# First block's heads: two latent tiles normalized ahead, the last tile's split and stores on two engines each, and attention that waits for its operands head by head

## The reference

```python
proj = jnp.einsum('bsd,dc->bsc', h, w_in[l])
cq, ckv, kr = proj[..., :o1], proj[..., o1:o2], proj[..., o2:o3]      # 384, 256, 32 columns
dq, dk, dv = proj[..., o3:o4], proj[..., o4:o5], proj[..., o5:]       # 8 heads of 64 each
q  = einsum('bsr,rc->bsc', rms_norm(cq, g_q[l]), w_uq[l])             # 8 heads of 96
kv = einsum('bsr,rc->bsc', rms_norm(ckv, g_kv[l]), w_ukv[l])          # 8 heads of 64 + 64
# rotations of the last 32 columns of q, of kr, and of the first 16 of each head of dq and dk
out_a = mla_attention(q, k, v)
out_b = dilated_attention(partial_rope(dq), partial_rope(dk), dv)
```

## Time and profile before

| | |
|---|---|
| time, median of 3 runs | 4233.45 us (4229.98 to 4238.81) |
| profiled execution's own time | 4241.43 us |
| its span, first to last instruction | 4239.6 us |
| busy PE, DVE, ACT, POOL | 3618.3, 2504.6, 2043.9, 782.3 us |
| mean granted clock of TensorE | 0.926 of full |
| `stage_heads1`, first load to the next stage's first | 324.55 to 477.02 us |
| first attention's loads to its first matmul | 477.02 to 490.96 us |
| first matmul of the second block's first attention | 2289.95 us |

### The profile page before, as it was taken

How to read it: one execution, slowest core, us unless ns; L and a number is a source line. 1 busy time by engine, 2 the same in 40 slices (tenths; PEclk the granted TensorE clock), 3 DMA queues, 4 the chain that set the end, 5 groups by cost and what they waited for, 6 DMA issues and landing times. The chain is left out here.

```text
span 4239.6 us, 68993 instructions
## 1 busy us (share of the span) xinstructions
PE 3618.3 (85%) x24823; PEld 2980.6 (70%) x24823; DVE 2504.6 (59%) x4458; ACT 2043.9 (48%) x3629; POOL 782.3 (18%) x464
## 2 busy tenths in 40 slices
PE   3996699988659999759997899965979997899759
PEld 3993488776548888648886677854768786788647
DVE  1204366433577888557653777755647745877655
ACT  1315455751047777552223666654442225666542
POOL 0212200020026665413340000002013430000020
PEclk7998799999679999879998999997989998999989
DMA  7126643412869999643234434341233326244413
GB/s 278 58 72 225 195 119 68 87 42 74 342 255 388 396 396 396 228 162 102 88 103 115 137 78 88 65 98 54 79 131 113 109 85 190 56 92 92 85 56 96
DMA packets 425466, 624.68 MB, mean 147 GB/s; under 512 B 118693, under 2 KB 281157, under 8 KB 424101
## 3 DMA queue, kind: packets, MB, share of 16 engines
q1 hardware_dynamic: 413216, 576.55, 43.8%
q0 software_dynamic: 8096, 30.02, 2.4%
q10 hardware_dynamic: 3812, 13.69, 1.0%
HBM read 486.20 MB, written 133.97 MB: 146 GB/s over the span
## 5 line engine op out<-in xcount | busy, mean ns | idle before, releaser
L1230 ACT ACTIVATE aa_prob<-aa_ps,aa_nm 128x256 f32<-128x256 f32 (+2 forms) x680 | 473.5, 696 | 287.0 <-DVEq L1181 248.9
L1101 PE MATMUL aa_ps<-aa_op 128*128 128x512 f32 (+2 forms) x1408 | 376.0, 380 | 177.9 <-DVEq L1189 130.4
L1180 DVE TENSOR_REDUCE aa_nm<-aa_ps 128x1 f32<-128x1280 f32 (+1 forms) x252 | 345.9, 1373 | 227.4 <-PE aa_ps L1101 214.6
L1101 PEld LDWEIGHTS aa_ps<-aa_op 128*128 128x128 f32 x1408 | 235.8, 193 | 298.7 <-issue 158.6
L1989 PE MATMUL pr_ps<-pr_wH,hT_part 128*128 128x512 f32 (+1 forms) x1120 | 429.5, 383 | 0.0
L1721 ACT ACTIVATE ex_high<-ex_ring 128x2048 fp32r<-128x2048 f32 x192 | 368.7, 1920 | 98.3 <-PE ex_pg L1697 43.2
L1767 DVE TENSOR_TENSOR ex_ring_part<-ex_ring,ex_high 128x2048 fp32r<-128x2048 f32 x144 | 377.1, 2619 | 52.4 <-ACTq L1722 40.6
L1131 PE MATMUL aa_po<-aa_pT,aa_op 128*64 128x128 f32 x5552 | 388.7, 282 | 0.0
L1989 PE MATMUL pr_ps<-pr_wH,x_sb_part 128*128 128x512 f32 x896 | 361.1, 403 | 24.4 <-DVEq L2065 20.5
L1112 PE MATMUL aa_ps<-ident,aa_prob 128*128 128x128 f32 x2776 | 376.4, 279 | 6.1 <-ACTq L1234 5.9
L1989 PE MATMUL pr_ps<-pr_ws_part,x_sb_part 128*128 128x512 f32 x896 | 354.0, 395 | 0.0
(11 more groups left out here) (298 smaller groups left out, 6984.9 us busy)
## 6 DMA issues: line engine op xcount, KB each, us to landing
ex_ring<-in_w_gate SPq DMA_DIRECT2D x64, 1024.0 KB, 9.9
ex_ring<-in_w_up SPq DMA_DIRECT2D x64, 1024.0 KB, 8.3
ex_ring<-in_w_down SPq DMA_DIRECT2D x64, 1024.0 KB, 8.0
aa_op<-z_d SPq DMA_DIRECT2D x120, 320.0 KB, 9.5
z_d<-pr_zT SPq DMA_DIRECT2D x120, 256.0 KB, 2.8
pr_ws<-in_w_in SPq DMA_DIRECT2D x14, 2048.0 KB, 8.7
mod_w<-in_w_ada SPq DMA_DIRECT2D x10, 2048.0 KB, 13.4
rt_mw<-in_w_ada SPq DMA_DIRECT2D x8, 2048.0 KB, 16.5
```

What stands on the lines that cost most here:

```text
L1101: mm = tensor.matmul(ps[:, base[h] + at:base[h] + at + m], q.bitcast(F32R), kk.bitcast(F32R), start=i == 0, stop=i == len(ab) - 1)
L1180: vector.tensor_reduce(most, scores[:, 0:g_.count[t]], AX.X, ALU.max, negate=True)
L1230: scalar.activation(prob[:, base[h] + c0:base[h] + c1], ps[:, base[h] + c0:base[h] + c1], ACT.Exp, bias=nm[:, h % 4:h % 4 + 1], scale=-1.0 ...
```

## The change

In `stage_heads1` the scaled latents get a second buffer, and tile t + 2 is normalized in pass t: ACT's `latents(t + 2)` stands behind `turned_latents(t + 1)` and ahead of `finished(t - 1)`, DVE's behind `heads(t)`. `load(1)` moves ahead of the gains and weights. For the last tile DVE makes the LOW parts of groups 1 and 3, and ACT issues the stores of groups 2 and 3. In `stage_attention` each head of a unit has a semaphore of its own.

```diff
-            c_n, c_T = sb("cn", [P, Q_RANK + KV_RANK]), sb("cT", [P, CR, P])
+            c_n, c_T = sb("cn", [P, 2, Q_RANK + KV_RANK]), sb("cT", [P, CR, P])
...
                     if t == 0:
                         load(0)
+                        load(1)
...
-                        load(1)
                     if t + 2 < ST:
...
-                            sp.wait_ge(low, (t - 1) * 4 + m + 1)
+                            if t < ST:
+                                sp.wait_ge(low, (t - 1) * 4 + m + 1)
+                            elif m < 2:
+                                sp.wait_ge(low if m == 0 else low_last, (ST - 1) * 4 + 1 if m == 0 else 1)
+                            else:
+                                continue
...
-                    if t:
-                        dve.wait_ge(cT_ps, t)
+                    if t >= 2:
+                        dve.wait_ge(cT_ps, t - 1)
...
                 latents(0)
                 dilated(0)
+                latents(1)
                 for t in range(ST):
-                    if t + 1 < ST:
-                        latents(t + 1)
                     heads(t)
+                    if t + 2 < ST:
+                        latents(t + 2)
                     if t + 1 < ST:
                         dilated(t + 1)
+
+                for m in (1, 3):
+                    dve.wait_ge(high, (ST - 1) * 4 + m + 1)
+                    o = outT[m][:, (ST - 1) % 2]
+                    vector.tensor_tensor(o[:, LOW].bitcast(F32R), o[:, LOW], o[:, HIGH], ALU.subtract)
+                    dve.drain().then_inc(low_last, 1)
...
                 latents(0)
+                latents(1)
                 act.wait_ge(gains, 32)
                 turned_latents(0)
                 for t in range(ST):
-                    if t + 1 < ST:
-                        latents(t + 1)
                     key_value(t)
                     if t + 1 < ST:
                         turned_latents(t + 1)
+                    if t + 2 < ST:
+                        latents(t + 2)
                     if t:
                         finished(t - 1)
                 finished(ST - 1)
+                tok = slice((ST - 1) * P, ST * P)
+                for m, dst in ((2, q_dil), (3, k_dil)):
+                    act.wait_ge(low if m == 2 else low_last, (ST - 1) * 4 + 2 if m == 2 else 2)
+                    for x in (HIGH, LOW):
+                        act.dma_start(dst[x].rearrange("(c p) s -> p c s", p=P)[:, :, tok], outT[m][:, (ST - 1) % 2, x])\
+                            .then_inc(t_st[(ST - 1) % 2], 16)
...
-                    for m in range(4):
+                    for m in range(4) if t < ST - 1 else (0, 2):
...
-        loaded = [sum(16 * g_.n_loads for g_, _ in units[u % 2:u + 1:2]) for u in range(len(units))]
+        loaded = [sum(8 * g_.n_loads for g_, _ in units[u % 2:u + 1:2]) for u in range(len(units))]
...
-                    if t == 0 and j == 0:
-                        pe.wait_ge(ld[u % 2], loaded[u])
+                    if t == 0:
+                        pe.wait_ge(ld[u % 2][j], loaded[u])
```

More of the change, by code:

```diff
@@ L651, in stage_heads1 @@
             sem(n + s) for s in ("_sq", "_cn", "_cps", "_csb", "_kvup", "_qup", "_qout", "_qk", "_dil", "_tr"))
-        ev, cp, high, low = (sem(n + s) for s in ("_ev", "_cp", "_high", "_low"))
+        ev, cp, high, low, low_last = (sem(n + s) for s in ("_ev", "_cp", "_high", "_low", "_lowlast"))
         v_st, t_st = ([sem(f"{n}_{s}{j}") for j in range(2)] for s in ("vst", "tst"))
@@ L724, in latents @@
                     rstd(dve, var, root, ss[:, :], rt[:, :], r[:, :], tm[:, :], t + 1)
-                    if t:
-                        dve.wait_ge(cT_ps, t)
-                    vector.tensor_scalar(c_n[:, 0:Q_RANK], x[:, 0:Q_RANK], r[:, 0:1], None, ALU.mult)
-                    vector.tensor_scalar(c_n[:, Q_RANK:], x[:, Q_RANK:Q_RANK + KV_RANK], r[:, 1:2], None, ALU.mult)
+                    if t >= 2:
+                        dve.wait_ge(cT_ps, t - 1)
+                    vector.tensor_scalar(c_n[:, t % 2, 0:Q_RANK], x[:, 0:Q_RANK], r[:, 0:1], None, ALU.mult)
+                    vector.tensor_scalar(c_n[:, t % 2, Q_RANK:], x[:, Q_RANK:Q_RANK + KV_RANK], r[:, 1:2], None, ALU.mult)
                     dve.drain().then_inc(cn, 1)
@@ L840, in latents @@
                     for c in range(CR):
-                        mm = tensor.transpose(cps[:, c, :], c_n[:, c * P:(c + 1) * P], ident[:, :])
+                        mm = tensor.transpose(cps[:, c, :], c_n[:, t % 2, c * P:(c + 1) * P], ident[:, :])
                     mm.then_inc(cT_ps, 1)
@@ L980, in tiles_at @@
             return [m for m in range(M) if 2 * m + lag[2 * m] + behind == s]
-        ld, lv = ([sem(f"{name}_{s}{b}") for b in range(2)] for s in ("ld", "lv"))
+        lv = [sem(f"{name}_lv{b}") for b in range(2)]
+        ld = [[sem(f"{name}_ld{b}{j}") for j in range(2)] for b in range(2)]
         ex0, tr0 = sem(f"{name}_ex0"), sem(f"{name}_tr0")
@@ L1026, in operands @@
                         for x in (HIGH, LOW):
-                            yield qT(g_, b, x, j, slice(0, g_.dq)), q_[x][:, j, :]
-                            yield kT(g_, b, x, j, slice(0, g_.dq)), k_[x][j]
+                            yield j, qT(g_, b, x, j, slice(0, g_.dq)), q_[x][:, j, :]
+                            yield j, kT(g_, b, x, j, slice(0, g_.dq)), k_[x][j]
                         continue
@@ L1032, in operands @@
                         rows = slice(m * g_.dq, (m + 1) * g_.dq)
-                        yield qT(g_, b, 0, j, rows), q_[qx][:, j, :]
-                        yield kT(g_, b, 0, j, rows), k_[kx][j]
+                        yield j, qT(g_, b, 0, j, rows), q_[qx][:, j, :]
+                        yield j, kT(g_, b, 0, j, rows), k_[kx][j]
                         if g_.dq == 64:
-                            yield kL(g_, b, j, rows), k_[LOW][j]
+                            yield j, kL(g_, b, j, rows), k_[LOW][j]
             def value_operands(u):
@@ L1055, in loads @@
                 def loads(u):
-                    for dst, src in itertools.islice(operands(u), 0, None, 1 if u else 2):
-                        sp.dma_start(dst, src).then_inc(ld[u % 2], 16)
+                    for j, dst, src in itertools.islice(operands(u), 0, None, 1 if u else 2):
+                        sp.dma_start(dst, src).then_inc(ld[u % 2][j], 16)
                     for dst, src in value_operands(u):
@@ L1234, in exponentials @@
                         act.drain().then_inc((ex0, ex)[x], 1)
-                for dst, src in itertools.islice(operands(0), 1, None, 2):
-                    act.dma_start(dst, src).then_inc(ld[0], 16)
+                for j, dst, src in itertools.islice(operands(0), 1, None, 2):
+                    act.dma_start(dst, src).then_inc(ld[0][j], 16)
                 for s in slots:
```

## The result

The changed kernel takes 4264.64 us (median of 5 runs, 4258.12 to 4270.21), the kernel before 4234.98 us (5 runs, 4229.98 to 4239.14). The ratio is 1.0064, with a 95% interval of 1.0052 to 1.0075: 27 us slower, 22 to 32 (the two medians are 29.7 us apart). The profiled execution took 4260.41 us.

A forecast was written before the change was run, and what follows sets the result against it. Before, ACT's list plus its wait for transposes bounds a pass; changed, a load-store loop does. 36.3 + 6.2 - 2.1 - 0.9 + 0 - 7.8 = +31.7 on 4233.45 gives 4265 us; 8-in-10 range 4250 to 4277.

The forecast's parts named there:

- The closed loop: Stage's tile passes: squares wait for a load behind stores that wait for ACT; four passes of 24.4 us, +36.3 us.
- The choice of 5.20: In the loop: ACT's copies of `finished` taken as 5.20 us, not 4.13, because PE would have stood before them.
- The margin before: Stage's passes before the change: the tile load was hidden with some 2 us to spare.
- The start: Stage's start: weights land later behind `load(1)`, root waits for DVE's heads, copies slower as PE cools; +6.2 us.
- The last two passes: Tiles 5 and 6, with no latents ahead: passes of 14.0 and 11.4 us, -2.1 and -0.9 us.
- The tail: Last tile's split and stores: the DMA queue is already full, so 0 us.
- Head by head: Attention: head 0 starts earlier but only one block of scores is won at each of three waits; -7.8 us.
- The rival on the other side: Loop: pipelining works if the load lands under 9 us after the HIGH copies; -15 to -20 us, 4215; chance 3%.
- Half hidden: Loop: shorter wait through faster issues from a rested queue; passes 18 to 20 us, 4238 to 4248; chance 9%.
- The dearer loop: Loop: PE's products at half clock add 1 to 3 us a pass; 4270 to 4280; chance 12%.

The follow-up runs named there:

- e3_tail_only: The kernel before with only the last tile's LOW-part subtractions and stores split over two engines each: 4237.85 us, ratio 1.0000.
- e4_loop_only: The kernel before with only the latents two tiles ahead and tile 1's load ahead of the weights: 4275.21 us, ratio 1.0089.
- e9_five_buffers: The changed kernel with five tile buffers, loads ahead of stores, squares before turned latents, DVE's latents before heads, start order mostly restored: 4217.64 us, ratio 0.9949 to kernel before.
- e5_behind: The changed kernel with ACT's squares and root of tile t + 2 behind the copies of tile t - 1: 4226.74 us, ratio 0.9980 to the kernel before.

## Why the prediction was right, step by step

- **The closed loop** was the step that carried it: 24.4 us a pass in four passes, +36.3. Measured 24.35, +36.1. Taken apart: issue of the load 10.60 for 10.61, from there to the squares 6.61 for 6.6, squares and root 1.83 for 1.91, copies 5.31 for 5.20. (The four terms of the forecast add up to 24.32, which it rounds up to 24.4.) The choice of 5.20 held: of the two lengths in rows 3, 4.13 came at a granted clock of 1.00 and 5.20 at 0.50, and in the slow pass it was 0.54. The wait itself was put too short, 8.2 to 8.7 us against a stated 4 to 8, because ACT was ready for the squares 8.5 to 9.0 us after the HIGH copies, the early end of what was allowed; in a pass that the load sets, this costs nothing. The margin before was smaller than the forecast's 2 us: the load of tile 5, issued at 389.81, took 6.7 us and was wanted at 397.39, 0.9 us later. That it is this loop, and not DVE's heads or the queue's fill, rests on three runs: with all four loads ahead of the stores the four waits go, with two of them two go, and with the squares behind the copies none is left.
- **The start**: +6.2 forecast, +5.4 measured (365.40 - 321.18 against 363.37 - 324.55). Of it the products' start +2.5 for +2.5 (336.03 - 321.18 = 14.85 against 12.38). The copies took 4.74 us, between the two lengths I had, at a granted clock of 0.64. That leaves 2.3 us for DVE's heads ahead of the root, for 2.7. The products' first row:

```profile
336.03 6.42 PE L884 MATMUL hd_pk<-hd_wukv,hd_cT 128*128 128x512 f32 x8 [4.44 <-DMA hd_wuq<-in_w_uq]
```

- **The last two passes**: 14.0 and 11.4 forecast, 14.54 and 12.03 measured, so -1.6 and -0.3 in place of -2.1 and -0.9. This comparison rests on two profiles at unlike clocks; with a clock near 1.00 in both (`e3_tail_only` 15.04 and 11.02, `e4_loop_only` 13.05 and 11.03) the two terms are -2.0 and 0. The stage in sum: +39.5 forecast, +39.8 measured. That the two meet within 0.3 us is luck, since the stage before took 150.5 to 152.5 us from profile to profile.
- **The tail** at 0: 15.44 us from the last HIGH copies to attention's loads, 15.32 before, and a ratio of 1.0000 with the part alone. The Trainium skill, "DMA: Bandwidth & Descriptors", section "Issuing engines are not separate DMA queues", says that starting transfers from several engines saves only the time that the sequencer takes to start them; the trace agrees, 15.44 us with two of the groups on ACT's queue against 15.32.
- **Head by head**: -7.8 forecast, -11 measured in the run of the part alone, within the stated 4 to 10 only by its interval. The mechanism (one block of scores, not the whole early start) is shown; the sizes were off both ways: in the first attention the first product with the values comes 26.6 us after the loads in the changed kernel (27.4 in the part alone) and 28.4 before, 1.0 to 1.8 for 2.4; in the second block's it is 3.3 and, in the last, 3.0 for 2.7. All that lay in front was won there, since DVE and ACT were through with head 0 before head 1 arrived. By these rows the sum is 7.3 to 8.1, close to the forecast; the rest of the -11 lies within its interval.
- **One thing expected of the profile did not come**: ACT's wait for the transposes was to shrink, and it stayed at 20.3 us of 21.6. I had put it down to DVE's scaling being late. With that out of the way PE's products, late in their turn, stand in its place.
- **The rival on the other side** (the pipelining works, about 4215) failed on its condition, as I had it: the load lands 17.2 us after the HIGH copies, not under 9. But its price was wrong. With the loads there in time the passes were 17.1 us, not shorter than before, and the kernel was level with before. It took the squares in another place, with the other edits of `e9_five_buffers`, to bring a pass to 14 us.
- **The rivals near the forecast.** Half hidden (18 to 20 us a pass) asked for faster issues from a rested queue. The queue did rest: the DMA share was 0.54 over the slow passes, 0.74 to 0.89 before. The issue came after 10.60 us all the same, and the load landed in 6.5 to 6.6. The dearer loop wanted PE's branch through 17 us after the HIGH copies; it was through, and ACT ready for the squares, after 8.5 to 9.0.
- **The total** of 4265 against 4264.64 is closer than the parts deserve. The loop and the start alone cost +38 for a forecast +39.5, attention brought -11 for -7.8, and against the kernel run beside it the change is +27, with +31.7 forecast: all inside the intervals, and no better known than by some 5 us.

## What to carry to other kernels

When a consumer is moved a pass ahead, follow its data back through every in-order queue to where they are issued; if the issue stands behind something that waits for work behind the moved consumer, a new closed loop sets the pass, and its length can be added up from the rows of the kernel before. Moving an item earlier in one engine's list is a change for all that it is now in front of: put it where that engine waits anyway. And a queue that is full when all engines are idle, as at this stage's end, gave nothing for earlier or divided issues.

## What the hardware showed that I had not expected

Two sizes. The path through POOL and SP repeats to 0.1 us: in eight instances (363.37 to 373.98 in the kernel before, 365.40 to 376.00 in the changed one, and so on) HIGH copies to the load's issue took 10.60 to 10.63 us, with the passes at 15 or at 24 us. And DVE's root was slow in one place: a TENSOR_TENSOR of 128x2 took 1.15 us while POOL subtracted, and 0.16 without it, as the next rows of `e5_behind` show. It ended at 386.07, with POOL's instruction, which ended at 386.05. In the kernel before four of the eight instances of this line took 1.14 or 1.15 us, all four beside POOL's subtractions, and the other four 0.16; so this was there before the change and is part of the 2.6 us for which ACT stood.

```profile
384.77 1.28 POOL L907 TENSOR_TENSOR hd_oT<-hd_oT 128x512 fp32r<-128x512 f32 x1
384.92 1.15 DVE L353 TENSOR_TENSOR hd_tm<-hd_tm,hd_ss 128x2 f32<-128x2 f32 x1
...
386.39 0.16 DVE L357 TENSOR_TENSOR hd_r<-hd_r,hd_tm 128x2 f32<-128x2 f32 x1
```
